# Eight gate products of the last merge pass moved into the differential attention of a hybrid encoder layer

## What is computed

```
def gated_merge(h, branches, merge_w, merge_b, branch_up):
    out = None
    for i, y in enumerate(branches):
        term = jax.nn.sigmoid(h @ merge_w[i] + merge_b[i]) * (y @ branch_up[i])
        out = term if out is None else out + term
    return out
```

## Time and profile before

| | |
|---|---|
| median of 3 runs | 2191.21 us (2190.84 to 2196.25) |
| profiled execution | 2191.2 us, span 2189.5 us |
| TensorE (PE) busy | 1970.5 us, 90% |
| VectorE (DVE) busy | 1413.4 us, 65% |
| ScalarE (ACT) busy | 1111.6 us, 51% |
| GpSimd (POOL) busy | 270.8 us, 12% |
| mean granted TensorE clock | 0.968 |

### The profile page before, as it was taken

The page is one execution under the profiler, slowest core; times in us unless marked ns, Lnnn a source line. Parts: engine busy times, 40 slices in busy tenths (PEclk is TensorE's granted clock), DMA queues, the critical chain, the costliest instruction groups (busy, mean ns, idle before and its releaser), DMA issues. The chain is left out here.

```text
span 2189.5 us, 32211 instructions
## 1 busy us (share of the span) xinstructions
PE 1970.5 (90%) x12704; PEld 1188.9 (54%) x12704; DVE 1413.4 (65%) x1789; ACT 1111.6 (51%) x1602; POOL 270.8 (12%) x263
## 2 busy tenths in 40 slices
PE   5998999899998988899999999999599999999981
PEld 3455465555543546788447875578345445444440
DVE  5446533589974686544333374543689999999995
ACT  4462323466656431112423353343578888888863
POOL 1010000000100443341120000000100111111103
PEclk9999999999999999999999999999799999999995
DMA  4410101211001252221411241051599999999966
GB/s 166 161 49 29 36 23 58 73 44 49 25 25 44 88 181 75 85 59 35 164 44 49 77 141 39 6 182 44 205 363 422 423 422 422 422 422 422 422 272 240
DMA packets 138215, 356.21 MB, mean 163 GB/s; under 512 B 37968, under 2 KB 91376, under 8 KB 111472
## 3 DMA queue, kind: packets, MB, share of 16 engines
q1 hardware_dynamic: 94304, 273.27, 32.9%
q10 hardware_dynamic: 34944, 48.24, 6.4%
q0 software_dynamic: 8848, 33.03, 3.9%
HBM read 305.75 MB, written 44.56 MB: 160 GB/s over the span
## 5 line engine op out<-in xcount | busy, mean ns | idle before, releaser
L730 PE MATMUL psum<-arena 128*128 128x512 f16 (+2 forms) x6000 | 1017.5, 328 | 15.1 <-ACT arena L1301 5.4
L730 PEld LDWEIGHTS psum<-arena 128*128 128x128 f16 x6000 | 572.6, 99 | 402.2 <-issue 25.5
L1133 PE MATMUL psum<-arena 128*128 128x512 f16 x2304 | 513.9, 382 | 13.0 <-issue 9.9
L689 DVE SCALAR_TENSOR_TENSOR arena<-arena 128x2048 f16<-128x2048 f32 x192 | 437.2, 2285 | 66.6 <-ACT arena L684 66.4
L684 ACT ACTIVATE arena<-arena 128x2048 f16<-128x2048 f32 x192 | 365.3, 1908 | 65.6 <-DMA arena<-in_w_dram 35.2
L1133 PEld LDWEIGHTS psum<-arena 128*128 128x128 f16 x2304 | 224.9, 98 | 279.9 <-issue 21.3
L1853 DVE SCALAR_TENSOR_TENSOR arena<-arena 128x512 f16<-128x512 f32 (+1 forms) x212 | 141.4, 686 | 129.4 <-ACT arena L1283 129.1
L2703 POOL DMA_INDIRECT arena<-xhat,arena x32 | 65.8, 2056 | 849.2 <-PE psum L1122 446.5
L1283 ACT ACTIVATE arena<-arena 128x512 f16<-128x512 f32 (+1 forms) x212 | 127.0, 616 | 44.2 <-issue 11.5
L2600 POOL TENSOR_TENSOR arena<-arena 128x512 f32<-128x512 f32 x48 | 66.3, 1381 | 581.9 <-DVE arena L1872 581.9
L1301 ACT ACTIVATE arena<-psum,arena 128x512 f32<-128x512 f32 x64 | 43.8, 684 | 150.4 <-PE psum L730 150.1
(11 more groups left out here) (382 smaller groups left out, 2188.4 us busy)
## 6 DMA issues: line engine op xcount, KB each, us to landing
arena<-in_w_dram SPq DMA_DIRECT2D x192, 1024.0 KB, 11.9
arena<-in_merge_w_dram SPq DMA_DIRECT2D x64, 256.0 KB, 3.3
yrows<-arena ACTq DMA_DIRECT2D x32, 512.0 KB, 7.8
arena<-in_w_in_dram SPq DMA_DIRECT2D x48, 256.0 KB, 2.8
gdn_lq<-arena ACTq DMA_DIRECT2D x8, 1024.0 KB, 4.2
arena<-gdn_lq ACTq DMA_DIRECT2D x8, 1024.0 KB, 5.0
arena<-in_xattn_wkv_dram SPq DMA_DIRECT2D x32, 256.0 KB, 2.9
yrows<-arena POOLq DMA_DIRECT2D x1, 7680.0 KB, 24.4
```

What stands on the lines that cost most here:

```text
L689: nc.vector.scalar_tensor_tensor(half_of(XW[m][1], half), half_of(XLAND[m], half), WS, half_of(XW[m][0], half), ALU.mult, ALU.subtract).th ...
L730: mm = nc.tensor.matmul(bank[prt[0]:prt[1], c0:c1], lhs[a](k), rhs[b](k), start=(k == 0 and a + b == 0), stop=(k == nk - 1 and a == 1))
L1133: mm = nc.tensor.matmul(PS[:, bank, :], left[a][:, k, :], right[b][:, k, columns], start=k + a + b == 0, stop=(k == n - 1 and a == 1))
```

## The change

Tiles 2 to 5 of pass 3 (`EARLY`) lose their gate products there. Two new panels, early1 and early2, each with four gate groups of 16 parts in all and 4 chunks, follow merge0 in the attention, and every unit gets one part more (112 parts for 32 units). Panels merge31 and merge32 are gone; between merge30 and merge33 stands one panel, late3, of the eight up products of tiles 2 to 5, with 2 chunks (four blocks of k). ScalarE stores each early tanh to DRAM behind its own tanh (8 stores of 256 KB). At "x_again" it loads all eight back, ahead of x, into memory that `MP` uses later. VectorE waits for all of them at the up products of tiles 2 to 5. "merged_pair" of tile j-1 now stands behind the second up product of tile j, for j from 2 to 5.

```diff
+EARLY = (2, 3, 4, 5)
+LATE = (0, 3)
...
-        for q in range(4):
+        for q in range(4) if i != 3 else LATE:
...
+            if (i, q) == (3, 0):
+                add("late3", [(up[:, :, 128 * j:128 * j + 256], j - EARLY[0], 0) for j in EARLY[::2]],
+                    [("up", 3, j, half) for j in EARLY for half in range(2)])
+
+    def early(*qs):
+        for q in qs:
+            add(f"early{q}", [(kview(A["merge_w"][3])[:, :, q * 256:q * 256 + 256], 0, 0)],
+                [("gate", 3, 2 * q + jt, half) for jt in range(2) for half in range(2)])
...
     merge(0)
+    early(1, 2)
...
-                    if kind == ("gate", 3, kind[-2], 0) and kind[-2] and part == 2:
+                    if kind == ("gate", 3, kind[-2], 0) and kind[-2] not in (0,) + EARLY and part == 2:
                         steps.append(("merged_pair", kind[-2] - 1))
+                    if kind[:2] == ("up", 3) and kind[2] in EARLY and kind[3] == 1:
+                        steps.append(("merged_pair", kind[2] - 1))
...
-        diff += [None] + [("diff_comb", u + 1)] * more + [("diff_pv", u)] + [None] * (u % 2)
-    dense(*merge(0), between=diff)
+        diff += [None] + [("diff_comb", u + 1)] * more + [("diff_pv", u)] + [None] * (1 + u % 2)
+    dense(*merge(0), *[f"early{q}" for q in (1, 2)], between=diff)
...
+        early = [n for n in gates if kind_of[n][1] == 3 and kind_of[n][2] in EARLY]
+
+        def early_gate(kind):
+            return f32(BR + 4096 * kind[3] + 512 * kind[2], 512)
...
-                        if gate_no[n] >= 2:
+                        slot = gate_no[n] % 2
+                        if gate_no[n] >= 2 and gates[gate_no[n] - 2] in early:
+                            act.wait_ge(gate_out[slot], 16 * sum(m < n and gate_no[m] % 2 == slot for m in early))
+                        elif gate_no[n] >= 2:
                             act.wait_ge(*counter("vec_evac").at(up_of(gates[gate_no[n] - 2])))
...
+                        if n in early:
+                            act.wait_ge(*e.at(n))
+                            S.dma_start(A["early_gates"][early.index(n)], SG[slot]).then_inc(gate_out[slot], 16)
...
+                    for s in range(2):
+                        act.wait_ge(gate_out[s], 16 * len(early) // 2)
+                    for m, n in enumerate(early):
+                        S.dma_start(early_gate(kind_of[n]), A["early_gates"][m]).then_inc(gate_in, 16)
                     for tt in range(TT):
                         S.dma_start(X[:, tt, :], A["x"][tt * P:tt * P + P, :]).then_inc(x_again, 16)
...
-                        dve.wait_ge(*counter("act_evac").at(gate_of(n)))
+                        gate = SG[gate_no[gate_of(n)] % 2]
+                        if gate_of(n) in early:
+                            gate = early_gate(kind)
+                            dve.wait_ge(gate_in, 16 * len(early))
+                        else:
+                            dve.wait_ge(*counter("act_evac").at(gate_of(n)))
```

More of the change, by code:

```diff
@@ L208, in dense @@
             order.extend(steps)
-    merge = lambda i: [f"merge{i}{q}" for q in range(4)]
+    merge = lambda i: [f"merge{i}{q}" for q in range(4)] if i != 3 else ["merge30", "late3"] + [f"merge3{q}" for q in LATE[1:]]
     order.append(("norm_stats", "x", 0))
@@ L260, in plan_schedule @@
                 gdn += [("gdn_load", i + 1), ("gdn_load_inv", i + 1)]
-    dense("nq", "nk", "nv", *merge(2), between=gdn)
+    dense("nq", "nk", "nv", *merge(2), *[f"early{q}" for q in ()], between=gdn)
     dense("nz", between=[("fin", "gdn")])
@@ L583, in products @@
                 j = kind[2] % 2
-                return [((0, P), (0, 512), wt(j * P, j * P + P, KT),
+                k0 = 2 * (kind[2] // 2) - EARLY[0] if kind[1] == 3 and kind[2] in EARLY else KT
+                return [((0, P), (0, 512), wt(j * P, j * P + P, k0),
                          act(Y[YSLOT[kind[1]]], kind[3] * 512, kind[3] * 512 + 512), 2)]
@@ L619, in up_of @@
             return g_of[("up",) + kind_of[n][1:]]
+        early = [n for n in gates if kind_of[n][1] == 3 and kind_of[n][2] in EARLY]
+        def early_gate(kind):
+            return f32(BR + 4096 * kind[3] + 512 * kind[2], 512)
+        gate_out = [sem(f"early_gate_out{s}") for s in range(2)]
+        gate_in = sem("early_gates_in")
         par_in = sem("params_in")
@@ L1871, in _ @@
                                 dve.wait_ge(*counter("pool_merge").at(adds[add_no[n] - 2]))
-                        V.scalar_tensor_tensor(dst, SG[gate_no[gate_of(n)] % 2], 1.0, bank, ALU.add, ALU.mult).then_inc(*e.mark(n))
+                        V.scalar_tensor_tensor(dst, gate, 1.0, bank, ALU.add, ALU.mult).then_inc(*e.mark(n))
                     elif name in ("mix", "wo"):
@@ L2772, in program @@
         A["gdn_lq"] = nc.dram_tensor("gdn_lq", (TT, P, 2048), F32, kind="Internal").ap()
+        A["early_gates"] = nc.dram_tensor("early_gates", (2 * len(EARLY), P, 512), F32, kind="Internal").ap()
         A["gdn_diag"] = nc.dram_tensor("gdn_diag", (2, 32, 4096), F32, kind="Internal").ap()
```

## The result

The changed kernel takes 2205.21 us, median of 7 runs (2198.66 to 2207.95), beside 2191.21 us for the kernel before (7 runs, 2188.42 to 2197.42). The ratio is 1.0054, 95% interval 1.0038 to 1.0070: slower by more than 0.3%, where 2183.9 us was forecast and 2174 to 2195 was the range.

What follows compares the result with a forecast made beforehand. TensorE, busy 90% of the span, was taken as the bound, with some 20 us of holes in the attention. -41.4 + 23.2 + 3.3 + 2.2 + 4.9 + 0.5 = -7.3 us from 2191.2 gave 2183.9, range 2174 to 2195.

Steps and rivals of the forecast that it cites:

- 32 parts removed: Last pass: 8 gates of 4 parts leave TensorE's unbroken stretch, 1.295 us each, -41.4 us.
- Residual waits in the attention: Attention: TensorE waits left after the added parts fill holes, 6 us, between 0 and 24.2.
- The growth of the stage: Attention: 41.4 us added, less 24.2 of old waits, plus 6 of residual waits, +23.2 us.
- 16 issues: Reload in the last pass: ScalarE's sixteen load issues delay the tanh TensorE awaits, gap 4.65 us, +3.3, at most +4.6.
- Clock behind the gap: Last pass: after the longer reload gap TensorE runs at half clock for a while, +2.2 us (1.65 to 2.7).
- Up panel: Last pass, eight up products in a row: VectorE starts late and needs longer than TensorE, +4.9, plus 0.5 for clock.
- rival 2: Up panel slower through VectorE-GpSimd blocking or ScalarE's pair copies, and slower issues: +3.3 to +7, 2187 to 2191 us; chance 0.18.
- Stores: Attention: the eight 256 KB tanh stores delay ScalarE only, and waits for them should be over in time; no separate term.
- The rest: Everything behind the last pass's first mix product was expected unchanged, 0 us.
- Rival 1: Attention absorbs nothing, grows by 41.4 us; change costs +10.9, 2202 us; 13.3 us of residual wait decides the sign; chance 0.12.
- the signs that I named against myself: Three-part units over 7 us as a rule, a transfer ending any TensorE wait, or clock at 0.5 over the up panel.

Runs made afterwards that it cites:

- add_after_comb: Changed kernel with GpSimd's addition of an up product that falls between a unit's scores and combination waiting for that combination: 2195.69 us, attention 223.49 instead of 227.78.
- comb_first: Changed kernel with the next unit's exponentials and combination ordered ahead of this unit's first part and value product: 2192.95 us, attention 218.63 instead of 227.78.
- x_on_sp: Changed kernel with the eight loads of x issued by SyncE, after sixteen parts of the panel, instead of by ScalarE: 2198.26 us, last pass 73.76 instead of 80.24.
- no_reload: Changed kernel without the eight tanh stores, their eight loads and the waits on them (output incomplete): 2192.95 us, last pass 73.59 instead of 80.24.
- stats_later: Changed kernel with the two sums of squares of mem moved behind the panel of eight up products: 2202.91 us, last pass 77.41 instead of 80.24.
- narrow_late: Changed kernel with GpSimd's eight additions in the up panel narrowed to one column of 512 (output incomplete): 2197.69 us, last pass 75.28 instead of 80.24.
- combo2: combo with the conversion pairs of tiles 1 to 4 moved from the up products into the last gate panel: 2181.99 us, last pass 66.95 instead of 71.29.
- combo: Changed kernel with comb_first, x_on_sp and stats_later together: 2181.82 us, ratio 0.9957 to the kernel before.

## Why the prediction was wrong

From 2189.5 to 2200.3 the span grew by 10.8 where -7.3 was forecast: 18.1 us to explain. By the steps of the sum:

- **32 parts removed, -41.4: right.** The last pass lost 41.4 and got back 4.45 (gap) + 2.65 (clock behind it) + 7.9 (up panel), which gives -26.4; measured -26.3. What came back belongs to the steps below.
- **Residual waits in the attention, 6 us: the step that failed. Measured 18.8.** TensorE's own work is 15 x (6.32 + 7.61) = 209.0 us, and the stage took 227.78, of which 14.3 is idle time by the view of its waits. Two short units waited 3.6 each: both hold a tanh, a conversion and an up product, where I had put +1.9 on one and +1.2 on the other. Without GpSimd's addition (add_after_comb) they still wait 2.55, so the addition that I had left out of the loop is 1.0 us of it, and the sum of the three other steps was 0.65 too small. Three long units, the last of a head, waited 1.2 to 1.4 each: VectorE scales the next head's bias there ahead of this unit's low copies, which I took as hidden by the four parts. The low clock behind the second wait of 3.40 is 1.5. Over the other units 6.2 are spread. comb_first shows that half of the 18.8 is the order: with the next unit's exponentials and combination put first 9.6 are left, which is still above my 6. The growth of the stage is 31.7, and 33.0 with the part that the last unit gained behind it, and not 23.2: 9.8 us. That is less than the 12.8 us of waits missed, since the added part of the first unit lies ahead of the stage (whose start moved by 0.3 only) and TensorE's own work per unit was about 0.06 us shorter than I had taken.
- **16 issues, +3.3: 4.45, so 1.2 us too small.** The mechanism was right (gap ended by that tanh; x_on_sp and no_reload take it away). The issues of x went from 0.48 to 0.62 us each behind the eight gate loads, inside the bound of +4.6 that I had named.
- **Clock behind the gap, +2.2: 2.65.** Right within 0.5.
- **Up panel, +5.4 with its clock: 7.9.** The late start by the sums of squares was right (stats_later -2.8), but I read the 0.4 us by which the additions of the earlier trace rows are longer as a mild mutual slowing. It was only the rest of a VectorE operation already running: in the trace of before one such addition starts at 1062.60 beside a conversion that runs from 1062.43 to 1063.12, and it ends 1.13 us after that conversion. Where longer operations met, the wait was longer. The Trainium skill (SBUF — State Buffer, Who interferes with whom) calls the port pair that VectorE's operations with two SBUF inputs share with GpSimd an exclusive lock. The trace after agrees: L1884 took 1.75 instead of 0.69, L2362 1.91 instead of 1.23, L2214 1.25 instead of 0.22 us, and narrow_late and combo2 give the time back from either side. This is rival 2's mechanism; its price alone, +2.5, would not have changed the sign.
- **Stores, 0: 0.5 us, and 1.4 of clock beside it**, not in the attention but behind it, at the last tanh, where ScalarE's next work is what the recurrence waits for. The stretch grew by 3.2, of which 1.3 is the last unit's added part. It has 3.4 us more at a granted clock of 0.50 than before; add_after_comb, with the same stores, has 3.4 us less, so the clock's share is not a price of the stores.
- **The rest, 0: 1.9**, and 0.3 before the attention. The rest varies by more than that between kernels that are alike in it, so nothing shows that this is the change.

The conversion beside the first addition of the earlier trace rows, timeline of VectorE before:

```profile
1062.43 0.68 DVE L1853 SCALAR_TENSOR_TENSOR arena<-arena 128x512 f16<-128x512 f32 x1
```

9.8 + 4.2 (last pass) + 1.9 + 1.9 + 0.3 = 18.1. Rival 1 ended where the result is, +10.9 against 10.8, and that is chance. Of residual waits it needed 13.3 us to turn the sign, and there were 18.8; but its reason, that each unit keeps its waits and the stage grows by 41.4, is not what happened. The stage grew by 33.0, the waits sit in some units where several things meet, and the other 8 us came from terms that rival 1 had as I had them or at nothing. Of the signs that I named against myself none came whole: the clock was low at the end of the up panel, but not over it; 4 of the 15 units of three parts took over 7 us, but not as a rule; and none of the transfers that I had named ended a wait of TensorE.

What stays open: which of the many small waits make up the 6.2 us, why equal waits once lose the clock and once not (some 1.7 us each time, in several stages), and whether combo2 is faster than combo as a whole.

## What to carry to other kernels

Work moved into a stage with idle TensorE time is worth what the loop of the other engines leaves, unit by unit: lay every small job on its unit and look at the worst ones, since two of them waited 7.2 us here. Put what the next unit waits for first in the in-order queues, before work is added; here that order was worth 4 us alone and 9 with the added work. DMA issues and sums that nobody waits for don't belong in front of the one tanh that TensorE waits for, and such fixed costs took more than half of what half a move had taken away (11.1 of 20.7 us).

## What the hardware showed that I had not expected

- A VectorE operation with both inputs in SBUF on 128 x 1 elements took 1.25 us instead of 0.22 beside an addition of GpSimd that began 0.03 us earlier.
- Two gaps of TensorE of the same 3.40 us: behind the one at 483.73 the clock stayed at 2.4 GHz, behind the one at 560.78 it was 1.2 GHz. In stats_later, where these units are the same, it was 1.2 GHz behind both. Windows of 1 us, after:

```profile
484.00:485.00 1.00, 1.00 (x10) 0.84 (x9) 1.00 (x3) 0.58 (x2) 0.00 (x0) 1.00 0.00 0
...
561.00:562.00 1.00, 1.00 (x6) 1.00 (x6) 1.00 (x3) 0.07 (x1) 0.00 (x0) 0.50 0.00 0
562.00:563.00 1.00, 1.00 (x6) 0.66 (x5) 1.00 (x3) 0.74 (x2) 0.00 (x0) 0.50 0.05 16
```

- Issues of x on ScalarE took 0.62 us each behind eight other loads, 0.48 without them.
